# Banded keys, values and queries projected first, rotary arithmetic beside the banded gate, decay differences by one VectorE addition

## The reference

```
proj = h @ w_in
(dn_q, dn_k, dn_v, dn_z, dn_beta, dn_decay, sw_q, sw_k, sw_v, sw_z) = split(proj)
dn = gated_deltanet_bidir(dn_q, dn_k, dn_v, dn_beta, dn_decay, conv_w, a_log, dt_bias)
dn = rms_norm(dn) * silu(dn_z)
sw = windowed_gqa_with_sinks(sw_q, sw_k, sw_v, ...) * silu(sw_z)
x = x + concat([dn, sw]) @ w_out
```

```
decay = exp(where(incl, g[:, None] - g[None, :], -inf))
m     = where(strict, (k_beta @ k.T) * decay, 0);  t_inv = inverse(eye + m)
a     = where(incl, (q @ k.T) * decay, 0)
```

## Time and profile before

| | |
|---|---|
| median of three runs | 1079.17 us (1077.08 to 1079.38) |
| the profiled execution | 1081.45 us, of which the span of instructions is 1079.5 us |
| TensorE busy | 999.3 us, 93% of the span |
| VectorE, ScalarE, GpSimd busy | 486.9, 454.8, 438.2 us |
| share of the chain that ended last | PE 75%, DVE 13%, ACT 6%, POOL 4% |

### The profile page before, as it was taken

One profiled execution on the slowest core, in us unless ns is written; L12 is line 12 of the kernel. 1 busy time (PEld: TensorE's weight loads), 2 busy tenths in 40 slices (PEclk: granted clock), 3 DMA queues, 4 the chain that ended last, 5 costly groups with the idle time before them and its releaser, 6 DMA issues.

```text
span 1079.5 us, 12926 instructions
## 1 busy us (share of the span) xinstructions
PE 999.3 (93%) x5270; PEld 837.2 (78%) x5270; DVE 486.9 (45%) x808; ACT 454.8 (42%) x815; POOL 438.2 (41%) x245
## 2 busy tenths in 40 slices
PE   4998997769999899989998989989999999999987
PEld 4887885658889889778686767788888888888876
DVE  5453253377666626242426633333333333564434
ACT  5444751523446225244366552353434343432223
POOL 2432691630002055343468744253434444444440
PEclk9999998789999999999999999999999999999998
DMA  7322231000000003522412212233232323233302
GB/s 273 117 62 90 91 93 40 1 1 1 1 1 1 1 1 138 168 94 66 133 58 62 77 59 78 58 103 113 82 114 78 117 78 117 79 116 95 97 25 79
DMA packets 24011, 82.52 MB, mean 76 GB/s; under 512 B 2736, under 2 KB 2992, under 8 KB 23824
## 3 DMA queue, kind: packets, MB, share of 16 engines
q1 hardware_dynamic: 23088, 80.05, 23.3%
q10 hardware_dynamic: 864, 1.64, 0.4%
HBM read 77.48 MB, written 2.10 MB: 74 GB/s over the span
## 4 chain that ended last, share of the span: by engine, by line
PE 75%; DVE 13%; ACT 6%; POOL 4%; issue 1%; DMA 1%; DVEq 0%; ACTq 0%; POOLq 0%
PE bank L1837 71%; PE bank L1845 4%; DVE qk L1406 2%; DVE vc L1406 1%; ACT wh L1088 1%; DVE xs L1406 1%; DVE r L1400 1%; DVE xl L1400 1%; ACT qk L1088 1%; DVE mp L1400 1%; POOL wl L987 1%; DVE swr L1400 1%; ACT xs L1088 1%; ACT L1088 1%; ACT xh L1088 1%
## 5 line engine op out<-in xcount | busy, mean ns | idle before, releaser
L987 POOL TENSOR_TENSOR wl<-raw,wh 128x1024 fp32r<-128x1024 f32 (+1 forms) x131 | 315.5, 2413 | 409.8 <-ACT wh L1088 409.7
L1837 PE MATMUL bank<-xh,wh 128*128 128x512 f32 (+1 forms) x544 | 209.4, 385 | 4.8 <-DVE xl L1400 4.8
L1837 PE MATMUL bank<-xh,wl 128*128 128x512 f32 (+1 forms) x544 | 207.8, 382 | 0.0
L1837 PE MATMUL bank<-xl,wh 128*128 128x512 f32 (+1 forms) x544 | 207.8, 382 | 0.0
L1088 ACT ACTIVATE wh<-raw 128x1024 fp32r<-128x1024 f32 (+1 forms) x131 | 135.6, 1042 | 125.1 <-PE bank L1837 124.7
L1837 PE MATMUL bank<-wh,xh 128*128 128x512 f32 (+1 forms) x352 | 139.9, 398 | 9.7 <-DVE xl L1400 6.8
L1837 PE MATMUL bank<-wh,xl 128*128 128x512 f32 (+1 forms) x352 | 134.9, 383 | 0.0
L1837 PE MATMUL bank<-wl,xh 128*128 128x512 f32 (+1 forms) x352 | 134.6, 382 | 0.0
L1837 PEld LDWEIGHTS bank<-xh,wh 128*128 128x128 f32 x544 | 103.8, 191 | 24.2 <-issue 3.8
L1837 PEld LDWEIGHTS bank<-xh,wl 128*128 128x128 f32 x544 | 103.5, 190 | 19.7
L1837 PEld LDWEIGHTS bank<-xl,wh 128*128 128x128 f32 x544 | 103.7, 191 | 18.8
(11 more groups left out here) (242 smaller groups left out, 1553.2 us busy)
## 6 DMA issues: line engine op xcount, KB each, us to landing
raw<-in_wflat SPq DMA_DIRECT2D x127, 512.0 KB, 3.5
h<-in_x SPq DMA_DIRECT2D x4, 512.0 KB, 5.4
h<-in_x SPq DMA_DIRECT2D x1, 2048.0 KB, 9.6
gain<-in_pr SPq DMA_DIRECT2D x3, 512.0 KB, 3.7
consts<-in_cf SPq DMA_DIRECT2D x1, 1472.0 KB, 9.5
raw<-in_wflat SPq DMA_DIRECT2D x4, 272.0 KB, 2.6
kh<-kh SPq DMA_DIRECT2D x8, 128.0 KB, 2.3
kl<-kl SPq DMA_DIRECT2D x8, 128.0 KB, 2.3
```

The source lines that it names most:

```text
L987: e.tensor_tensor(WL[u % NS][:, 0:n], RAW[u % NS][:, 0:n], WH[u % NS][:, 0:n].bitcast(F32), ALU.subtract).then_inc(w_lo.up(u), 1)
L1837: return e.matmul(o, l, r_, start=start, stop=stop, skip_group_check=part)
```

## The change

The order of the units changes: kv and q come first, ahead of the twelve `ch` units, then sz and z. The steps of `gates` now stand in the loop over the `ch` units behind the second and fourth of them, and the squares and the root of `swa_prep` behind the fifth to the ninth. The rotary arithmetic stands behind the four sz units, and a new generator `rope_turn` holds the five `rope_t`, between the transposes of v and of k. Two `gc` steps of chunk 0 are taken between z units.

The decay difference is now one VectorE addition of the bank and the negated column for either direction, followed by Abs and Exp on ScalarE. The absolute difference is symmetric, so `ee` need not be turned: the eight groups of four transposes go, and `at` is q k times `ee`, both directions out of one bank, with the triangular mask put on by GpSimd afterwards (`inv_turn_mask`, as the step `inv_mt` of GpSimd). The scan waits for GpSimd's mask in place of VectorE's product.

```diff
+    tok1 = [("w_in", range(k, k + 2), cols, sum(w for _, w in cols)) for cols in P1_TOK for k in range(0, 8, 2)]
+    plan += tok1[:8]
     for c in P1_CH:
         plan.append(("w_in", range(8), [c], 128))
+    plan += tok1[8:]
...
+    U_KV, U_Q, U_CH, U_SZ = 0, 4, 8, 20
...
+    for u0, by in ((U_KV, lambda tb: (proj, ("v", tb))), (U_Q, lambda tb: (proj, ("q", tb)))):
+        for tb in range(4):
+            G.take(("tok", u0, tb), by(tb))
+        for i in range(4):
+            w_ahead(u0 + i + 2)
+            do("tok", u0, i, "n0", SLOT0, 272 if u0 == U_KV else 512)
...
+    g2, g3 = gates(), swa_prep()
+    for j in range(12):
+        w_ahead(U_CH + j + 2)
+        G.take(("ch", U_CH + j), (conv_v, (j, 4)))
+        do("ch", U_CH + j, "n0", 1)
+        if j:
+            do("conv", j - 1)
+            if 2 <= j <= 9:
+                do("square", j - 2)
+        if j in (1, 3):
+            step(g2)
+        if 4 <= j < 9:
+            step(g3)
+    do("conv", 11)
     G.over((0, 1, 2, 3))
-    g1 = in_turn(qk_norm(), to_tokens())
+    g1 = in_turn(qk_norm(), to_tokens("v"), rope_turn(), to_tokens("k"))
...
-    tok_part(12, 272, lambda tb: (proj, ("v", tb)), (g1, 2))
-    g2 = gates()
-    tok_part(16, 512, lambda tb: (proj, ("q", tb)), (g1, 1), (g2, 1))
-    g3 = swa_prep()
-    tok_part(20, 512, lambda tb: (proj, ("sz", tb)), (g1, 3), (g2, 1), (g3, 3))
+    tok_part(U_SZ, 512, lambda tb: (proj, ("sz", tb)), (g3, 1), (g1, 3))
...
-        step(g1, 3)
-        step(g2, 1)
-        step(g3, 3)
-    for g in (g1, g2, g3):
-        while step(g):
-            pass
-    for e in range(4):
-        step(gi[e // 2])
+        step(g1, 4)
+        if k in (1, 2):
+            step(gi[0])
+    while step(g1):
+        pass
+    step(gi[1], 2)
...
+        def inv_turn_mask(cb):
+            for d in range(2):
+                at = h3(AT[cb][:, d, :])
+                on.wait_ge(*inv_v.at(("a0", cb, d)))
+                e.tensor_tensor(at, at, bc4(cf(("triU", "triL")[d])), ALU.mult).then_inc(inv_g.up(("a", cb, d)), 1)
...
         def inv_decay(cb, d):
             ee = WORK[cb]["EE"][d][:]
-            if d == 0:
...
-                for h in range(4):
-                    act(hs(ee, h), hs(psum[b], h), ACT.Relu, inv_a.up(("ee0", cb, d) if h == 3 else ("ee0", cb, d, h)),
-                        bias=NGC[:, d, cb, h:h + 1])
-            on.wait_ge(*(inv_v if d else inv_a).at(("ee0", cb, d)))
+            on.wait_ge(*inv_v.at(("ee0", cb, d)))
+            act(ee, ee, ACT.Abs, inv_a.up(("ee1", cb, d)))
+            on.wait_ge(*inv_a.at(("ee1", cb, d)))
             act(ee, ee, ACT.Exp, inv_a.up(("ee", cb, d)), scale=-1.0)
...
+            tt(h3(WORK[cb]["EE"][d][:]), h3(psum[b][:, :]), b4r(NGC[:, d, cb, :]), ALU.add, inv_v.up(("ee0", cb, d)))
...
             for d in range(2):
-                tt(h3(AT[cb][:, d, :]), h3(psum[b][:, :]), bc4(cf(("triU", "triL")[d])), ALU.mult, inv_v.up(("a0", cb, d)))
+                on.wait_ge(*inv_a.at(("ee", cb, d)))
+                tt(AT[cb][:, d, :], psum[b][:, :], WORK[cb]["EE"][d][:], ALU.mult, inv_v.up(("a0", cb, d)))
...
-            for d in range(2):
-                b, _ = BANK[("inv", cb, "ee", d)]
-                on.wait_ge(*inv_p.at(("ee", cb, d)))
-                on.wait_ge(*inv_v.at(("a0", cb, d)))
-                tt(AT[cb][:, d, :], AT[cb][:, d, :], psum[b][:, :], ALU.mult, inv_v.up(("a", cb, d)))
```

More of the change, by code:

```diff
@@ L471, in qk_norm, with to_tokens @@
                 yield
[L473 to L478, removed]
+    def to_tokens(what):
+        for cb in range(4):
+            G.take((what, cb), (tok_a, (what, cb)))
+            do("to_tok", what, cb)
+            yield
     def gates():
@@ L505, in invert @@
         for d in range(2):
-            take(("gc", d), (inv_a, ("ee0", cb, d)) if d == 0 else (inv_v, ("ee0", cb, d)))
+            take(("gc", d), (inv_v, ("ee0", cb, d)))
             do("inv_decay", cb, d)
@@ L1077, in gm_gain @@
             e.tensor_tensor(VG[:, tb, :], VG[:, tb, :], pr("gmlp_norm_g_2"), ALU.mult).then_inc(gm_g.up(("gain", tb)), 1)
-        return dict(prep=prep, qexp=qexp, rope_sq=rope_sq, inv_decay=inv_decay, inv_m=inv_m, z_gain=z_gain, swa_o=swa_o,
+        return dict(prep=prep, qexp=qexp, rope_sq=rope_sq, inv_decay=inv_decay, inv_m=inv_m, inv_mt=inv_turn_mask, z_gain=z_gain, swa_o=swa_o,
                     scan_keys=scan_keys, gm_w=gm_w, gm_sq=gm_sq, gm_gain=gm_gain, fa_norm=fa_norm)
@@ L1207, in tok @@
                         continue
-                    name, dst, f = {16: ("q", SWR[:, tb, 128:640], ACT.Copy), 20: ("sz", MIX[:, tb, 512:1024], ACT.Silu),
+                    name, dst, f = {U_Q: ("q", SWR[:, tb, 128:640], ACT.Copy), U_SZ: ("sz", MIX[:, tb, 512:1024], ACT.Silu),
                                     U_Z: ("z", MIX[:, tb, 0:512], ACT.Silu)}[u0]
@@ L1522, in inv_decay @@
         def inv_decay(cb, d):
-            if d:
-                ee = WORK[cb]["EE"][d][:]
-                b, _ = BANK[("inv", cb, "gc", d)]
-                on.wait_ge(*inv_p.at(("gc", cb, d)))
-                if cb in (1, 2):
-                    on.wait_ge(*dense.at((U_Z + 3, 3)))
-                for h in range(4):
-                    ts(hs(ee, h), hs(psum[b], h), GC[:, d, cb, h:h + 1], 0.0, ALU.subtract,
-                       inv_v.up(("ee0", cb, d) if h == 3 else ("ee0", cb, d, h)), ALU.max)
+            b, _ = BANK[("inv", cb, "gc", d)]
+            on.wait_ge(*inv_p.at(("gc", cb, d)))
+            on.wait_ge(*gate_v.at("ngc"))
+            if cb in (1, 2):
+                on.wait_ge(*dense.at((U_Z + 3, 3)))
+            tt(h3(WORK[cb]["EE"][d][:]), h3(psum[b][:, :]), b4r(NGC[:, d, cb, :]), ALU.add, inv_v.up(("ee0", cb, d)))
         def inv_kq(cb):
@@ L1991, in inv_kq @@
             t.then_inc(inv_p.up(("q", cb)), 1)
-        def inv_m(cb):
-            for d in range(2):
-                p = bank(("inv", cb, "ee", d))
-                on.wait_ge(*inv_a.at(("ee", cb, d)))
-                for h in range(4):
-                    t = tr(hs(p, h), sub(WORK[cb]["EE"][d], h))
-                t.then_inc(inv_p.up(("ee", cb, d)), 1)
         def inv_mt(cb):
@@ L2238, in tensor_engine @@
         return dict(split=split, ch=ch, ch_part=ch_part, tok=tok, tok_a=tok_a, tok_b=tok_b, last0=last0, last=last, pair=pair, qsum=qsum, to_tok=to_tok,
-                    gate2=gate2, rope_t=rope_t, inv_decay=inv_decay, inv_kq=inv_kq, inv_m=inv_m, inv_mt=inv_mt, inv_x=inv_x,
+                    gate2=gate2, rope_t=rope_t, inv_decay=inv_decay, inv_kq=inv_kq, inv_mt=inv_mt, inv_x=inv_x,
                     inv_d=inv_d, inv_x7=inv_x7, inv_t=inv_t, swa_s=swa_s, swa_t=swa_t, swa_o=swa_o, scan_keys=scan_keys, scan_v=scan_vn,
```

21 lines of the change are left out of this document (7 added, 14 removed).

## The result

| | before | after |
|---|---|---|
| median | 1078.81 us (6 runs, 1077.08 to 1083.26) | 1070.64 us (6 runs, 1069.04 to 1073.07) |
| ratio to before, 95% interval | | 0.991 [0.989, 0.993] |
| profiled execution | 1081.45 us | 1071.14 us |
| TensorE busy | 999.3 us | 989.7 us |

The change makes the kernel 0.9% faster, by 8.2 us in the medians and 10.3 in the profiled executions. The forecast was 1067.2 with a range of 1058 to 1076; the time lies inside, 3.4 us above the forecast. Measured by the profiled executions the miss is 1.6 us (12.0 forecast, 10.3 measured); the profiled execution of before stood 2.6 us above its median and that of after 0.5.

What follows compares the result with a forecast made beforehand. It took TensorE, 93% busy, to bound the kernel through its idle or slow stretches at 150 to 260 us. Gains 3.7 + 4.7 + 0.7 + 3.4 - 0.5 = 12.0 us gave 1067.2 against the median, range 1058 to 1076.

Steps and rivals of the forecast that it cites:

- rival 2: Inversion's start: `mp` and `dd` go at the pace of the attention pieces, gains 3.4 and 0.7 vanish: 1071.3 us; chance 0.11.
- rival 1: Convolution loop: table loads of gate1, gate2 and root cost as much again, 5.1 us: 1072.3; chance 0.16.
- `inv_m`: Four inversion chunks, `mp` to `dt`: 17.7 us instead of 21.1, gain 3.4; masks cost 0.5 in the last chunk.
- Start-up: Until the first projection matmul: a first unit 544 wide lets TensorE start 1.0 us earlier.
- The convolution loop: The `ch` units: gates, root and wider weights add 9.0 us to ScalarE's queue, leaving TensorE holes of 9.4.
- The rotary hole: TensorE's wait for `swr` before the z units, put at 9.1 us, goes away.
- Rival 3: End of the loop: gate and root hide in ScalarE's idle time, taps end 8 us earlier: 1059.2; chance 0.12.
- gc: Groups between z and k q: six left of eight, 5.3 us instead of 10.0, gain 4.7.
- k q to `mp`: Ahead of the first `mp`: Abs and Exp delay the attention exponential 0.8, warmer products give 1.5; gain 0.7 us.
- the rule: Skill's GpSimd contention: four `dd` behind the first mask grow 1.0 us each, total gain 8.5.
- the quiet reading: Masks on GpSimd don't slow the `dd` that way; total gain stays 12.0 us.
- rival 4: Gaps at loop's end hold TensorE at 1.2 GHz through sz and z; four cold units give 1084.7; chance 0.08.

Runs made afterwards that it cites:

- run 3: Changed kernel with gate1 moved behind the third q unit and gate2 ahead of the convolution loop, the root left in it: 1064.96 us, ratio 0.9863.
- run 4: `silu_next`: changed kernel with each convolution's silu issued behind the copy of the next convolution, gates and root still in the loop: 1060.32 us, ratio 0.9815.
- run 1: Changed kernel with the decay difference, turned `ee` and masks as before, so only the order changes: 1069.26 us, ratio 0.990 to before.
- run 2: Kernel before, in its old order, with only the new decay difference and its masks on GpSimd: 1074.18 us, ratio 0.9947 to before.
- run 9: Changed kernel with `gc`, Abs and Exp of chunks 1 and 2 issued behind the first k q products and two banded pieces: 1071.68 us, ratio 0.9912.
- run 5: Changed kernel with both `dd` products of a chunk waiting for GpSimd's second identity addition as well: 1072.43 us, ratio 0.9933.
- run 6: Changed kernel with GpSimd's triangular masks of `at` put six levels later: 1070.13 us, ratio 0.9898.
- run 8: Changed kernel with `dd` behind the `dt` products of the same chunk and the masks six levels later: 1158.39 us, ratio 1.0719.
- run 12: Changed kernel with silu behind the next convolution's copy, `dd` behind `dt` and the masks six levels later: 1150.49 us, ratio 1.0659.
- `dd_late`: Changed kernel with `dd` behind the `dt` products of the same chunk, masks left in place: 1070.22 us, ratio 0.9901.

## Why the prediction was right, and where it was off

The measured 1070.64 lies inside the range, but nearer to rival 2 (1071.3) and rival 1 (1072.3) than to the forecast of 1067.2. Stage by stage the terms up to k q held, that of `inv_m` failed, and two terms that nobody forecast made up part of it.

**Start-up: right.** 1.0 us was forecast, and 21.67 to 20.67 measured. The second `xs` took 2.17 us in place of the 3.18 of the earlier trace rows. No run tests this term alone.

**The convolution loop: right in its mechanism and its prices, and exact in the sum by luck.** Forecast and measured: gate1 4.8 and 4.2 us; gate2 1.7 and 1.8; the root 1.6 and 1.6; the start of the first `ch` unit 56.6 and 56.2; the end of the last taps 136.3 and 135.7; the low clock behind the holes 1.5 and 1.7. The new waits were put at 9.4 and are 7.5. The rotary hole of before was put at 9.1, as 9.9 less 0.8 for nine turns; the waits in it are 7.8, and its eight turns ran slowly and fill the other 2.1. The two errors, 1.9 and 1.3, nearly offset each other, and so the z units end at 189.9 as forecast. Runs 3 and 4 show the cause from two sides: take the gates out, or let the queue run on past the taps, and the holes go. They also show a term that the forecast left on the table: silu behind its own taps is what makes ScalarE's round 5.85 us.

**Rival 1, the table loads: wrong.** In the trace the instruction behind a load starts 1.30 us after it, as in before; the load back to silu lay beside the taps. The 2.66 us that the Trainium skill gives for a load with its drain ("ScalarE: Activation LUTs", "What ACT_TABLE_LOAD costs") are not seen in any round here: gate1's whole round grew by 4.2 with two loads exposed.

**Rival 3: not in this kernel.** ScalarE's idle time stayed inside the round, as the forecast held against it. Run 4 opened it: the last taps end at 126.5 us, 9.2 earlier, and the time is 1060.32 where rival 3 had 1059.2.

**gc: right.** 4.7 us were forecast, and 4.96 measured from z to k q.

**k q to `mp`: the clock gain was spent.** Forecast 0.7, measured 0.1. Two effects of 3.6 us each stand behind that small number. One is the warmer clock, which each half alone shows (15.0 us). The other is the wait for `pm` behind eleven Abs and Exp, which I had put at 0.8: it delays `pm` by 2.3 and lengthens TensorE's hole from 1.8 to 4.0, and the lower clock behind the hole costs 1.7 more. That these two cancel is worked out from the traces of runs 1 and 2; run 9, which should have freed the second, moved it elsewhere.

**`inv_m`: the step that failed.** Forecast 3.4 less 0.5 for the masks, measured 0.7. The forecast had each `dd` at 0.7 and a contention with the masks for the last chunk alone. In the run each pair lay beside GpSimd: beside the second identity addition in three chunks (2.34 us, 1.05 more than 1.29), beside additions and masks in the last (3.42, 2.1 more), 5.3 in all. In before the `at` product, which reads PSUM and kept its 0.68 us beside the addition, stood in just that place in three chunks of four; taking it out laid `dd` on the addition. The forecast looked for a mask beside a `dd` and passed over the pair of 2.02 us in the trace of before, which lies beside an addition. The chunk itself was put too long, since `dd` starts behind the first addition, 2.06 after `mp`, and not behind both; so only 2.2 of the 5.3 appear against the forecast. Runs 5 and 6 show both causes. The Trainium skill ("GPSIMD Engine Reference", section 8 "Key points") says that GpSimd contends with VectorE instructions that have two SBUF inputs. The trace agrees: a `dd` takes 1.74 us beside GpSimd and 0.69 alone, the factor of 2.5 that the forecast took from `xs`. The place was the identity addition first and the masks second. The sum that the forecast drew from the rule was 8.5; the gain was 9.5 at `dt` and 10.3 at the end, between that and the 12.0 of the quiet reading. Rival 2 said that the gain in `inv_m` and ahead of it would vanish. It nearly did (0.8 us of 4.1 were left), for another reason than the banded pieces that it named.

**What the forecast didn't have.** `dt` to `swo` gained another 1.9 us: over that stretch the clock was 1.00 and had been 0.89 before. The scan gained 1.1, at a clock of 0.91 where before had 0.83 in the same steps (from 354.6 and from 366 us, 20 us each). In the second block, which the change does not touch, 2.2 us were given back. 1.6 of them lie in one place, where TensorE is busy throughout at a lower clock, while before had 1.00 in the same steps:

```profile
519.60:527.60 8.00, 8.00 (x33) 6.33 (x33) 1.23 (x5) 2.40 (x5) 3.94 (x2) 0.80 0.32 99
```

Why it comes there was not settled; in `silu_next` it is missing, and that kernel is 1.6 us better off behind it.

**The sum.** 3.75 + 4.96 + 0.11 + 0.70 + 1.89 + 1.05 - 2.2 = 10.3 us in the profiled executions, where 12.0 was forecast. The forecast of slower by a cold clock through sz and z (rival 4) did not come: the clock was back 6 us behind the holes.

## What to carry to other kernels

Before you shorten what two engines do in turn, see what each removed operation was lying beside: a product out of PSUM had covered GpSimd's addition, and the SBUF product that took its place was slowed by it by 80%. In a strict queue, an operation that waits for another engine's answer to one issued just before belongs one round later; that single edit was worth as much as the whole change. Two edits that each warm the same stretch do not add up, so time each alone. And add up the waits before and after: here they came to 26 us both times, and what the change saved was matmul time.

## What the runs showed of the hardware that I had not expected

TensorE can stay at 1.2 GHz though it is never idle. In runs 8 and 12 it was busy for 100.00 of 100 us at a granted clock of 0.50 with the short matmuls of the inversion and the banded attention (128x64 to 128x384) one behind the other, from 241 to 439 us in run 8 and from 224 to 432 in run 12. In both the clock came back some 5 us after the work had changed to the products of `dt` and `mp`; whether for that reason is not shown. The kernel after does this work at a granted clock of 1.00 from 240 to 260 us. `dd_late` has both: three executions of 1067.91 to 1071.39 us at a mean clock of 0.98, and one of 1166.18 at 0.893.

Runs 8 and 12 share the packed stretch ahead. In each TensorE had been back at the full clock for some microseconds when it waited once more for `pm`, and the clock fell within 2 us of the end of that wait:

```profile
239.76 0.91 PE L1832 MATMUL bank<-skt,sqt 64*128 64x384 f32 x2 [1.56 <-ACT pm L1097]
221.93 0.91 PE L1834 MATMUL bank<-skt,sqt 64*128 64x384 f32 x2 [1.43 <-ACT pm L1097]
```

That this wait is the trigger is a guess and was not tested. It can't be enough by itself: the profiled execution of `dd_late` has a longer one, 3.71 us ahead of 234.98, and is at 1.00 from 240 us on. Why the clock then stays low through 190 us of busy time is open. It is a risk of some 90 us beside gains of 4.

A VectorE product of two SBUF operands, 0.69 us alone, took 1.74 us beside a GpSimd operation (`dd`), while the products out of PSUM (`dt`, four in 2.47, 0.68 each) were not slowed beside the masks. On GpSimd's side the additions kept their 1.27, but the two masks that lay beside the last `dd` pair took 3.39 together, 1.7 each, where the others took 1.27: both engines are slowed.
